# Thirty-two squares on ScalarE, cut into eight groups of four and set between the high parts of a gate block

## What is computed

```
n = rms_norm(h, norm1_g)
proj = n @ w_in
(q_att, c_kv, q_idx, k_idx, w_idx, r_q, r_k, r_v, r_gate, g_att, g_ret) = split(proj)
q = rms_norm(q_att.reshape(B, S, 8, 128), q_norm_g)      # needs the sum of squares of each head's 128 values
...
ret = retention_chunkwise(r_q, r_k, r_v, gammas)         # four heads
ret = group_norm_heads(ret, ret_norm_g)
y_ret = (silu(r_gate) * ret) @ w_ret_branch
```

## Time and profile before

| | us |
|---|---|
| median of three runs | 1610.09 (1609.7 to 1612.69) |
| the profiled execution, its own time | 1608.98 |
| its span, first to last instruction | 1607.1 |
| mean granted TensorE clock | 0.956 of full |
| TensorE busy | 1471.3 (92%) |
| VectorE busy | 1099.7 (68%) |
| ScalarE busy | 770.8 (48%) |
| GpSimd busy | 490.9 (31%) |

### The profile page before, as it was taken

How to read it: one execution, slowest core, us unless ns; L and a number is a source line. 1 busy time by engine, 2 the same in 40 slices (tenths; PEclk the granted TensorE clock), 3 DMA queues, 4 the chain that set the end, 5 groups by cost and what they waited for, 6 DMA issues and landing times.

```text
span 1607.1 us, 19862 instructions
## 1 busy us (share of the span) xinstructions
PE 1471.3 (92%) x7190; PEld 1215.8 (76%) x7190; DVE 1099.7 (68%) x1539; ACT 770.8 (48%) x1247; POOL 490.9 (31%) x365
## 2 busy tenths in 40 slices
PE   5989999997999896999998999999994789999996
PEld 5978788986889785677676888888883677777784
DVE  4339999999999567665469633346335777778884
ACT  5237223327231626776342442233253567778783
POOL 2310121371414044000234533222240243334431
PEclk9999999999999997999999999999996799999998
DMA  5210121112311012110354344443434787896865
GB/s 190 60 27 1 40 47 40 34 46 92 86 40 47 33 52 92 53 53 14 93 170 152 104 137 140 155 138 122 170 125 174 263 290 254 262 316 192 253 168 132
DMA packets 87217, 195.19 MB, mean 121 GB/s; under 512 B 11089, under 2 KB 32849, under 8 KB 84817
## 3 DMA queue, kind: packets, MB, share of 16 engines
q1 hardware_dynamic: 74448, 153.56, 29.2%
q0 software_dynamic: 8928, 32.51, 8.6%
q10 hardware_dynamic: 3744, 7.87, 1.3%
HBM read 200.71 MB, written 37.22 MB: 148 GB/s over the span
## 4 chain that ended last, share of the span: by engine, by line
PE 70%; DVE 11%; DMA 8%; ACT 4%; issue 3%; SPq 2%; POOL 1%; ACTq 0%; DVEq 0%; POOLq 0%
PE ps L710 19%; PE ps L711 19%; PE ps L712 19%; DMA e_raw<-in_w_up 6%; PE ps L933 4%; DVE dist L1568 2%; DVE e_lo L1950 2%; PE ps L923 2%; PE ps L1041 1%; ACT junk L1219 1%; DMA w_raw<-in_w_in 1%; SPq L690 1%; DMA xin<-in_x 1%; DVE f_sum L1686 1%; PE ps L875 1%
## 5 line engine op out<-in xcount | busy, mean ns | idle before, releaser
L2007 POOL TENSOR_TENSOR w_lo<-w_raw,w_hi 128x512 fp32r<-128x512 f32 (+1 forms) x184 | 254.9, 1390 | 626.1 <-ACT w_hi L1109 625.6
L1109 ACT CAST w_hi<-w_raw 128x512 fp32r<-128x512 f32 (+1 forms) x184 | 112.1, 615 | 429.6 <-PE ps L712 374.6
L710 PE MATMUL ps<-w_hi,n_hi 128*128 128x512 f32 (+2 forms) x704 | 245.5, 349 | 8.6 <-POOL w_lo L2007 6.8
L711 PE MATMUL ps<-w_lo,n_hi 128*128 128x512 f32 (+2 forms) x704 | 242.8, 345 | 0.0
L712 PE MATMUL ps<-w_hi,n_lo 128*128 128x512 f32 (+2 forms) x704 | 242.8, 345 | 0.0
L1950 DVE TENSOR_TENSOR e_lo<-e_raw,e_hi 128x2048 fp32r<-128x2048 f32 x93 | 210.1, 2286 | 29.3 <-ACT e_hi L1460 29.2
L1460 ACT CAST e_hi<-e_raw 128x2048 fp32r<-128x2048 f32 x93 | 176.1, 1914 | 66.2 <-DMA e_raw<-in_w_up 66.2
L1605 DVE MAX8 small<-dist 128x8 f32<-128x384 f32 (+5 forms) x192 | 171.8, 895 | 6.6
L710 PE MATMUL ps<-n_hi,w_hi 128*128 128x512 f32 x416 | 164.6, 396 | 7.5 <-POOL w_lo L2007 7.3
L1606 DVE MATCH_REPLACE8 dist<-small,dist 128x384 f32<-128x384 f32 (+5 forms) x192 | 168.1, 876 | 0.0
L711 PE MATMUL ps<-n_lo,w_hi 128*128 128x512 f32 x416 | 162.3, 390 | 0.0
(11 more groups left out here) (271 smaller groups left out, 2889.6 us busy)
## 6 DMA issues: line engine op xcount, KB each, us to landing
e_raw<-in_w_gate SPq DMA_DIRECT2D x62, 512.0 KB
e_raw<-in_w_up SPq DMA_DIRECT2D x62, 512.0 KB
e_raw<-in_w_down SPq DMA_DIRECT2D x31, 1024.0 KB
w_raw<-in_w_in SPq DMA_DIRECT2D x120, 256.0 KB, 2.7
a_raw<-att_dram SPq DMA_DIRECT2D x16, 512.0 KB, 3.6
a_raw<-ret_dram SPq DMA_DIRECT2D x16, 512.0 KB, 3.4
w_raw<-in_w_out SPq DMA_DIRECT2D x24, 256.0 KB, 2.9
w_raw<-in_w_in SPq DMA_DIRECT2D x40, 128.0 KB, 2.4
```

The source lines that it names most:

```text
L710: mm(out, a[0], b[0], start=first, stop=False, skip_group_check=skip)
L711: mm(out, a[0], b[1], start=False, stop=False, skip_group_check=skip)
L1109: nc.scalar.copy(w_hi[c % NH][:, :width], split_from(c)[:, :width]).then_inc(hi_ready, 1)
L2007: G.tensor_tensor(w_lo[c % NH][:, :width], split_from(c)[:, :width], w_hi[c % NH][:, :width].bitcast(F32), ALU.subtract).then_inc(lo_ready, 1)
```

## The change

`square_q0` takes a tile number and does the four squares of that tile. The call of all tiles behind `phase2` 1 goes. `out_block` no longer calls `ahead(name)` but writes its loop out, and in block `gate1` calls `square_q0(k)` after the high part of turn k, for k = 0 to 7. The count of instructions, their operands and their order among themselves stay.

```
-            def square_q0():
-
-                for t in range(NT):
-                    for h in range(4):
-                        col = S_QR + HA * t + h
-                        inst = A(junk2[:, h % 2 * P:(h % 2 + 1) * P], qst0[t][:, h * DH:(h + 1) * DH], ACT.Square,
-                                 accum_out=small[:, col:col + 1])
-                        if h == 3:
-                            inst.then_inc(q0_squares, 1)
-                            act.wait_ge(q0_squares, t + 1)
-                        else:
-                            seq(inst)
+            def square_q0(t):
+
+                for h in range(4):
+                    col = S_QR + HA * t + h
+                    inst = A(junk2[:, h % 2 * P:(h % 2 + 1) * P], qst0[t][:, h * DH:(h + 1) * DH], ACT.Square,
+                             accum_out=small[:, col:col + 1])
+                    if h == 3:
+                        inst.then_inc(q0_squares, 1)
+                        act.wait_ge(q0_squares, t + 1)
+                    else:
+                        seq(inst)
...
             def out_block(name):
-                ahead(name)
+                for k in range(KT):
+                    hi(number[name] * KT + k + NH - 1)
+                    if name == "gate1":
+                        square_q0(k)
                 kind, i = name[:-1], int(name[-1])
...
-                if (what, m) == ("phase2", 1):
-                    square_q0()
```

## The result

The changed kernel takes 1600.27 us, the median of nine runs (1596.06 to 1603.86); the kernel before takes 1609.3 us in nine runs of the same sessions (1606.15 to 1612.69). The ratio is 0.9943, with a 95% interval from 0.9929 to 0.9957: 9.2 us less (0.0057 x 1609.3), between 6.9 and 11.4. The forecast was 1602.2 us in a range from 1600.3 to 1605.0. The direction, the place and the mechanism were right; the time lies 0.03 us under the range. Two executions in the experiments, one of the kernel before (1755.57 us, clock 0.80) and one of one_piece (2466.59 us, clock 0.56), ran slow at a low granted clock and don't enter the ratios.

What follows compares the result with a forecast made beforehand. TensorE bounds the kernel and idles in gate1 because chunk 3's cast stands behind all squares on ScalarE. Gain 8.5 - 0.6 = 7.9 us, so 1610.09 - 7.9 = 1602.2 us, range 1600.3 to 1605.0.

Steps and rivals of the forecast that it cites:

- Part 1: Block gate1 from chunk 3: TensorE's stall goes, gaining 8.5 us, 6.95 idle and 1.5 slow clock.
- Parts 2 and 3: Within gate1: ScalarE's 2.36 us fits a 5.44 us turn; GpSimd's low parts come in time; nothing charged.
- Part 4: End of gate1: the eighth group of squares delays the Silu reads, giving back 0.6 us (0.1 to 0.9).
- Part 5: Behind gate1: next block starts 7.9 us earlier, all behind shifts as one; VectorE still waits 10 us.
- A: Inside gate1, part of the gain is lost, by table reloads or late GpSimd: 1603.8 to 1606.5 us, chance 0.06.
- B: Chunk 3's cast waits for something else, or time is given back later: 1607 to 1612 us, chance 0.03.
- C: Without the rest, TensorE gets the lower clock in the following 150 us: 1613 to 1646 us, chance 0.03.

Runs made afterwards that it cites:

- one_piece: Changed kernel with all 32 squares in one piece again, behind the cast of gate1's chunk 3: 1600.98 us, ratio 0.9958 to the kernel before.
- no_squares: Changed kernel with eight 4-column activations in place of the 64 square instructions, sums left out: 1597.2 us, ratio 0.9945 to the kernel before.
- two_per_turn: Changed kernel with two groups of squares in each of turns 0 to 3, none later: 1598.15 us, ratio 0.9935 to the kernel before.
- tail_one: Changed kernel with the eighth group of squares done twice, ahead of the Silu reads: 1599.77 us, ratio 0.9948 to the kernel before.
- tail_plus: Changed kernel with the eighth group of squares done three times, ahead of the Silu reads: 1604.43 us, ratio 0.9982 to the kernel before.
- before_again: Kernel before, unedited, run for a second profile: 1606.65 us, ratio 1.0004.
- before_third: Kernel before, unedited, run for a third profile: 1606.16 us, ratio 0.9993.

## Why the prediction was nearly right, and where it failed

**What bounds the kernel.** Right: the squares ahead of one cast were the wait, and nothing else had to be removed. no_squares and two_per_turn give the same stretch as after.

**Part 1, the stall.** 8.5 us of idle and clock. The whole stretch lost 8.47 us against the first profile of before, 8.9 to 9.0 against the two others, whose slow start lasted longer. From turn 0's first transposes to turn 1's it took 54.73 us, where the prediction has 419.05 - 364.33 = 54.72. The term was right for its own execution and was treated as fixed; it isn't.

**Parts 2 and 3, casts and GpSimd.** Right. The low part of chunk 4 ended at 391.87, which is 390.9 on the prediction's clock, for 390.5 forecast. The four row tiles that met VectorE's elementwise work (lines 1633 and 1634, 386.88 to 388.44) took 2.54 us for 2.17 of the next four, 0.4 us more, in the bounds of 0 to 1.5 and covered:

```profile
387.95 2.54 POOL L2081 TENSOR_SCALAR ro<-ro,small 128x256 f32<-128x256 f32 x4
390.57 1.30 POOL L2007 TENSOR_TENSOR w_lo<-w_raw,w_hi 128x512 fp32r<-128x512 f32 x1
391.85 2.17 POOL L2081 TENSOR_SCALAR ro<-ro,small 128x256 f32<-128x256 f32 x4
```

**Part 4, the tail. This term was mis-sized**: 0.6 us forecast, 0.01 measured (1.67 for 1.66). The pitch of the Silu reads when nothing holds them was taken as 0.575 us, between bounds of 0.52 and 0.64. It is (4.03 - 0.60) / 7 = 0.49, under the lower bound. TensorE fills a bank in 0.68 us, so from their late start at 417.09 the reads gain 0.19 us a bank; the fifth bank, the first that the transposes need, is free at 417.09 + 4 x 0.49 + 0.60 = 419.65, and they start at 419.99, 0.34 us later. Both bounds came from rows of the wrong kind. The casts read SBUF. The two copies that last 1.27 us together hold one pitch and one whole copy of 0.68 us, so their pitch is 0.59 and not half of 1.27, and they take their scale from a tile (`cst`), which the Silu reads don't. Whether that or the source makes the difference to 0.49 wasn't tested. There is also a slip in the sum: 420.8 + 0.42 is 421.2, not 421.3, so by its own pitch the term was 0.5 us. tail_one shows that the form of this step was right, since with the reserve used up the tail costs what it lasts.

**Part 5, behind the block.** Right: 181.7 us to the attention in all eleven profiles, VectorE's wait 9.34 us where about 10 were forecast.

**The sum and the range. Beside part 4, this is the step that put the time outside.** Of the 1.9 us between 1602.2 and 1600.27, 0.6 are part 4 and 0.8 the base, since the median of before went from 1610.09 in three runs to 1609.3 in nine. The remaining 0.5 us is as much as part 1 fell short in two of the three profiles of before, but also less than either kernel scatters, so it can't be assigned. The range took 1.9 us below the forecast from a spread of three runs and from a fixed gain, and what it names for it (1601.6, less 1.1) gives 1600.5, not 1600.3. That the median came out 0.03 us under the bound and not over it is chance. The runs of one kernel spread over 6.5 to 7.8 us here, and the profiles put most of it in the expert stage, which lasted from 354.7 to 363.8 us in the eleven profiles, whatever was changed 850 us earlier. What sets that stage's length from run to run was not tested. A range that had added this scatter to the bounds of the terms would have held the time.

**The rivals.** A: no table load appears in the block, and no turn was late; only its form (time lost at the tail) appears, in tail_plus and tail_one, with other work. B: the data was there, as the four casts had shown. C: the clock is 1.00 from 374 to 525 us without the rest, in both profiles of the change, so the mechanism didn't occur in most of the 150 us that it names. From 525 to 550 us it is 0.93 and 0.86, but there TensorE idles for 8 us, as in the kernel before (7.4 us, 0.86). What remains open is the short wait ahead of gate1. It lasts 1.63 to 1.65 us in all ten profiles that have it. Behind it the lower level was given in two of three profiles of before, and in none of the seven of the kernels that keep this wait and have the change in some form; what decides that was not found. After the change such a dip of 0.9 us would no longer be hidden. Whether it happens in other executions wasn't measured; moving the stores takes the wait away.

## What to carry to other kernels

Where one engine both feeds the bottleneck and does side work, put the feed first in each turn and cut the side work to what fits in its waits: here the cast's place gave three quarters of the gain and the cutting the rest. Look for the same pattern in work that isn't counted as busy: 4.5 us of DMA issue in the wrong place held TensorE up by 2.9 us here. And read the scatter of each stage before giving a range to a change of half a per cent.

## What the runs showed of the hardware

- Function Silu on 128 x 512 from PSUM lasts 0.60 us but back to back comes every 0.49 us (after and tail_plus, eight in 4.03 us), a good deal faster than the 0.68 us in which TensorE fills a bank with three matmuls.
- TensorE's clock after an idle stretch: at 1.38 us (tail_one) and 1.95 us (one_piece) it stayed at 1.00, at 3.12 us (tail_plus) it fell to the 1.2 GHz level for a while and cost 1.4 us, at 6 to 6.8 us (before) 1.5 to 2.0 us. At 1.63 to 1.65 us, ahead of gate1, it fell in two of ten profiles (before_again, before_third) and stayed in the others, so the length of the idle time alone doesn't decide. The Trainium skill (TensorE: Matmul & The Clock Gate, What's actually happening) says that the clock follows recent activity; the falls here all come behind a wait, which agrees, and the slow starts of 1.5 us behind an idle time of 6.8 us and of 1.9 to 2.0 us behind one of 6.0 us show that the cost isn't one figure.
